# Experts of 96 slots on plain float32 weights, with the tokens in four column tiles of TensorE

## The reference, cut to what matters

```python
D_MODEL = 1024; D_FF = 2816; N_EXPERTS = 8; TOP_K = 2
def swiglu(h, wg, wu, wd):
    g = jnp.einsum('btd,df->btf', h, wg)
    u = jnp.einsum('btd,df->btf', h, wu)
    return jnp.einsum('btf,fd->btd', jax.nn.silu(g) * u, wd)
def moe(h, router, wg, wu, wd):
    logits = jnp.einsum('btd,de->bte', h, router).astype(jnp.float32)
    vals, idx = lax.top_k(logits, TOP_K)
    gates = jax.nn.softmax(vals, axis=-1)
    comb = jnp.sum(jax.nn.one_hot(idx, N_EXPERTS, dtype=jnp.float32) * gates[..., None], axis=-2)
    out = jnp.zeros_like(h)
    for e in range(N_EXPERTS):
        out = out + comb[..., e:e + 1].astype(h.dtype) * swiglu(h, wg[e], wu[e], wd[e])
    return out
```

## Time and profile before

| | us |
|---|---|
| median of 3 runs (1280.49 to 1281.12) | 1280.8 |
| the profiled execution, first to last instruction | 1280.1 |
| attention and dense layer, up to the first expert matmul | 519.2 |
| first expert | 94.4 |
| each of the experts 2 to 7 | 94.3 |
| last expert | 92.8 |
| after its last matmul | 7.9 |

### The profile page before, as it was taken

The page is one execution under the profiler, slowest core; times in us unless marked ns, Lnnn a source line. Parts: engine busy times, 40 slices in busy tenths (PEclk is TensorE's granted clock), DMA queues, the critical chain, the costliest instruction groups (busy, mean ns, idle before and its releaser), DMA issues.

```text
span 1280.1 us, 18558 instructions
## 1 busy us (share of the span) xinstructions
PE 1262.4 (99%) x6937; PEld 1026.7 (80%) x6937; DVE 934.3 (73%) x888; ACT 803.0 (63%) x813; POOL 159.1 (12%) x175
## 2 busy tenths in 40 slices
PE   7999999999999999999999999999999999999998
PEld 5476699999974656788888888888888888888886
DVE  1667544443425667888888988988988988988897
ACT  2566533333324655767867877867867867777674
POOL 4131000000001020100310300400400400300300
PEclk9999999999999999999999999999999999999999
DMA  8261375445050624999999999999999999999994
GB/s 288 42 168 34 113 250 166 164 148 181 9 186 1 133 93 160 338 359 365 376 392 356 392 386 356 394 377 374 381 382 371 385 381 357 394 374 371 387 389 170
DMA packets 124595, 350.24 MB, mean 274 GB/s; under 512 B 8401, under 2 KB 33841, under 8 KB 124545
## 3 DMA queue, kind: packets, MB, share of 16 engines
q1 hardware_dynamic: 118896, 335.55, 71.9%
q0 software_dynamic: 4096, 12.43, 3.3%
q10 hardware_dynamic: 1552, 1.56, 0.4%
HBM read 340.57 MB, written 8.95 MB: 273 GB/s over the span
## 4 chain that ended last, share of the span: by engine, by line
PE 93%; DVE 3%; DMA 2%; ACT 1%; SPq 1%; issue 0%; DVEq 0%; ACTq 0%
PE ps L2337 38%; PE ps L2357 18%; PE ps L2244 11%; PE ps L1988 8%; PE ps L2260 5%; DMA ring<-in_w_in 2%; PE ps L2345 2%; PE ps L2061 1%; PE ps L2069 1%; PE ps L2121 1%; PE ps L2136 1%; PE ps L2174 1%; PE ps L2184 1%; PE ps L2001 1%; PE ps L2416 1%; PE ps L2085 1%
## 5 line engine op out<-in xcount | busy, mean ns | idle before, releaser
L1324 DVE TENSOR_TENSOR w_lo<-ring,w_hi 128x2048 fp32r<-128x2048 f32 (+1 forms) x322 | 675.2, 2124 | 178.8 <-ACT w_hi L938 176.4
L938 ACT ACTIVATE w_hi<-ring 128x2048 fp32r<-128x2048 f32 (+1 forms) x322 | 567.3, 1781 | 212.0 <-PE ps L2357 63.3
L2337 PE MATMUL ps<-w_hi,xg_hi 128*128 128x512 f32 (+1 forms) x768 | 287.8, 375 | 0.0
L2337 PE MATMUL ps<-w_hi,xg_lo 128*128 128x512 f32 (+1 forms) x768 | 286.1, 373 | 0.0
L2337 PE MATMUL ps<-w_lo,xg_hi 128*128 128x512 f32 (+1 forms) x768 | 285.4, 372 | 0.0
L2337 PEld LDWEIGHTS ps<-w_hi,xg_hi 128*128 128x128 f32 x768 | 144.6, 188 | 25.7
L2337 PEld LDWEIGHTS ps<-w_lo,xg_hi 128*128 128x128 f32 x768 | 144.2, 188 | 25.8
L2337 PEld LDWEIGHTS ps<-w_hi,xg_lo 128*128 128x128 f32 x768 | 144.6, 188 | 24.9
L2357 PE MATMUL ps<-w_hi,am_hi 128*128 128x512 f32 x340 | 133.7, 393 | 0.0
L2357 PE MATMUL ps<-w_lo,am_hi 128*128 128x512 f32 x340 | 132.5, 390 | 0.0
L2357 PE MATMUL ps<-w_hi,am_lo 128*128 128x512 f32 x340 | 132.3, 389 | 0.0
(11 more groups left out here) (357 smaller groups left out, 1435.2 us busy)
## 6 DMA issues: line engine op xcount, KB each, us to landing
ring<-in_moe_w_down SPq DMA_DIRECT2D x80, 1024.0 KB, 8.1
ring<-in_moe_w_gate SPq DMA_DIRECT2D x64, 1024.0 KB, 9.1
ring<-in_moe_w_up SPq DMA_DIRECT2D x64, 1024.0 KB, 9.4
ring<-in_moe_w_gate SPq DMA_DIRECT2D x32, 768.0 KB, 7.5
ring<-in_moe_w_up SPq DMA_DIRECT2D x32, 768.0 KB, 5.2
ring<-in_ffn_w_gate SPq DMA_DIRECT2D x11, 1024.0 KB, 7.4
ring<-in_ffn_w_up SPq DMA_DIRECT2D x11, 1024.0 KB, 5.3
ring<-in_ffn_w_down SPq DMA_DIRECT2D x10, 1024.0 KB, 5.2
```

The costliest lines, as they stand in the source:

```text
L938: A(hi[:, 0:size], src[:, 0:size], ACT.Copy).then_inc(hi_ready, 1)
L1324: V.tensor_tensor(lo[:, 0:size], src[:, 0:size], hi[:, 0:size].bitcast(F32), ALU.subtract).then_inc(lo_ready, 1)
L2337: ins = mm_(ps[:, b + c0 // 512, 0:c1 - c0], (xg_hi, xg_lo)[xp][:, k, :], w[wp][:, k % 2, c0:c1], start=(k == 0 and n == 0), stop=(k == KD ...
```

## The change

`SLOTS` becomes 96, three groups of 32 tokens. PE no longer takes split weights: tokens (`xg`, `am`) and weights are plain float32, straight out of the ring, which has 12 slots (`MOE_RING`: the six old ones and six in the place of the split pairs) with a semaphore each (`unit_in`); `unit_used`, raised by PE, tells that a unit was read. `lanes` does one k-row: TensorE is used as four column tiles of 32. Tiles 0 to 2 hold the three token groups and run over the first three quarters of the columns (`LANE_W`: 768, 768, 640; `D_LANE`: 768); tile 3 takes the rest of the columns (`TAIL`: 256, 256, 128; `D_TAIL`: 256) for each group in turn. Results of tile 3 stand on partitions 96 to 127, one group beside the other; `turned_parts` and the copies in `output` put them where they belong. The steps `wh` and `wl` of layer 1 (the first splits of expert weights) go, and so do `moe_events`, `moe_hi_part` and `moe_lo_part`. The first expert's rows are gathered with both parts summed in one bank, and transposed once. ACT and DVE each evacuate one of the two banks of turned activations and of turned tokens. `output` and `last_output` copy the tail columns over first and then scale. The dense layer keeps its split pairs and its ring.

```diff
-SLOTS = P
+GRAN = DEC
+MAIN = P // GRAN - 1
+SLOTS = MAIN * GRAN
...
+TAIL = [w // (MAIN + 1) // P * P for w in WIDTH]
+LANE_W = [w - t for w, t in zip(WIDTH, TAIL)]
+D_TAIL = D // (MAIN + 1)
+D_LANE = D - D_TAIL
...
-DENSE_PAIRS, MOE_PAIRS = 3, 4
+DENSE_PAIRS = 3
+MOE_RING = 12
...
-            for u in range(RING):
-                slot_room(last_in_slot[(MOE_AT + u) % RING])
+            for u in range(MOE_RING):
+                if u < RING:
+                    slot_room(last_in_slot[(MOE_AT + u) % RING])
+                elif u == RING:
+                    wait_full(sp, ("o", 1, len(GROUPS) - 1))
+                    sp.wait_ge(stored, 16 * DEPTH * 10)
                 load_unit(u, 0)
...
-                    sp.wait_ge(lo_ready, j * len(EXPERT) + (ND + u - RING + 1))
+                    sp.wait_ge(unit_used, j * len(EXPERT) + (u - MOE_RING + 1))
                     load_unit(u, e)
...
                 def output():
+
                     act.wait_ge(row_moved, j + 1)
-                    act.wait_ge(y_full, j + 1)
-                    A(y_out[:, :], wide(6), ACT.Copy, scale=slot_gate[:, 0:1]).then_inc(y_taken, 1)
+                    act.wait_ge(unit_used, j * len(EXPERT) + len(EXPERT))
+                    for g in range(MAIN):
+                        ins = A(y_out[GRAN * g:GRAN * g + GRAN, D_LANE:D], wide(6)[SLOTS:P, D_TAIL * g:D_TAIL * g + D_TAIL], ACT.Copy)
+                    ins.then_inc(y_tail, 1)
+                    A(y_out[0:SLOTS, 0:D_LANE], wide(6)[0:SLOTS, 0:D_LANE], ACT.Copy, scale=slot_gate[0:SLOTS, 0:1])
+                    act.wait_ge(y_tail, j + 1)
+                    A(y_out[0:SLOTS, D_LANE:D], y_out[0:SLOTS, D_LANE:D], ACT.Copy, scale=slot_gate[0:SLOTS, 0:1]).then_inc(y_taken, 1)
...
                 def wait_unit(u):
-                    pe.wait_ge(lo_ready, j * len(EXPERT) + (ND + u + 1))
+
+                    pe.wait_ge(unit_in[u % MOE_RING], j * MOE_FILLS + 16 * (u // MOE_RING + 1))
+
+                def lanes(b, x, w, main, tail, first, last):
+
+                    for c0 in range(0, main, 512):
+                        c1 = min(c0 + 512, main)
+                        for g in range(MAIN):
+                            ins = mm_(ps[GRAN * g:GRAN * g + GRAN, b + c0 // 512, 0:c1 - c0], x[:, GRAN * g:GRAN * g + GRAN], w[:, c0:c1],
+                                      start=first, stop=last)
+                        for g in range(MAIN):
+                            at_ = tail * g
+                            if c0 <= at_ < c1:
+                                ins = mm_(ps[SLOTS:P, b + c0 // 512, at_ - c0:at_ - c0 + tail], x[:, GRAN * g:GRAN * g + GRAN],
+                                          w[:, main:main + tail], start=(first and at_ == c0),
+                                          stop=(last and (g == MAIN - 1 or at_ + tail >= c1)))
+                    return ins
...
-                    w = [x[u % MOE_PAIRS][:, 0:2 * wd].rearrange("p (k c) -> p k c", k=2) for x in (w_hi, w_lo)]
+                    w = unit_at(u)[:, 0:2 * wd].rearrange("p (k c) -> p k c", k=2)
                     for k in (2 * h, 2 * h + 1):
-                        for c0 in range(0, wd, 512):
-                            c1 = min(c0 + 512, wd)
-                            for n, (wp, xp) in enumerate(PARTS):
-                                ins = mm_(ps[:, b + c0 // 512, 0:c1 - c0], (xg_hi, xg_lo)[xp][:, k, :], w[wp][:, k % 2, c0:c1],
-                                          start=(k == 0 and n == 0), stop=(k == KD - 1 and n == 2))
-                    in_use(ins, u)
+                        ins = lanes(0 if kind == "gate" else 2, xg[:, k, :], w[:, k % 2, :], LANE_W[c], TAIL[c], k == 0, k == KD - 1)
+                    ins.then_inc(unit_used, 1)
```

More of the change, by code:

```diff
@@ L200, in expert_plan @@
     return order + [("down", c, h) for c in (1, 2) for h in range(4)]
[L203 to L225, removed]
 def ffn_jobs():
@@ L442, in build @@
         w_ready = [sem(f"w_ready{i}") for i in range(RING)]
+        unit_in = [sem(f"unit_in{i}") for i in range(MOE_RING)]
+        unit_used = sem("unit_used")
         small_full = [sem(f"small_full{i}") for i in range(3)]
@@ L634, in build @@
         SPLIT_AT = (2, 3, 5)
-        DOWN_USED = 10
         def wait_pair(eng, n):
@@ L647, in dense_size, with unit_at @@
             return SLOT_W if key[0] != "down" or key[2] < 5 else SLOT_W // 2
[L649 to L667, removed]
+        def unit_at(u):
+            i = u % MOE_RING
+            return ring[:, (MOE_AT + i) % RING, :] if i < RING else ring_more[i - RING][:, :]
         GAINS_IN = 16 * len(GAIN)
@@ L944, in dense_hi_part @@
                 split_hi(ring[:, slot_of[key], :], n, w_hi[n % DENSE_PAIRS], dense_size(key))
[L946 to L954, removed]
-                split_hi(ring[:, s, :], u, w_hi[u % MOE_PAIRS], moe_size(u))
             def squares(l, t, where):
@@ L1278, in last_output @@
+                    act.wait_ge(y_tail, j + 1)
+                    A(y_out[0:SLOTS, D_LANE:D], y_out[0:SLOTS, D_LANE:D], ACT.Copy, scale=slot_gate[0:SLOTS, 0:1]).then_inc(y_taken, 1)
                 def last_output():
                     act.wait_ge(row_moved, j + 1)
-                    for half in range(2):
-                        act.wait_ge(y_half, half + 1)
-                        A(y_hi[:, 512 * half:512 * half + 512], ps[:, 6 + half, :], ACT.Copy, scale=slot_gate[:, 0:1]).then_inc(y_high, 1)
@@ L1284, in expert @@
-                for u in range(MOE_PAIRS, len(EXPERT) + MOE_PAIRS):
-                    for what, c in MOE_EVENTS.get(u, ()):
-                        if what == "silu":
-                            silu(c)
-                        elif what == "turned":
-                            chunk_high(c)
-                        elif what == "tokens" and not final:
-                            tokens_high(j + 2)
-                        elif what == "output":
-                            if final:
-                                last_output()
-                            else:
-                                output()
-                    if u < len(EXPERT) or not final:
-                        moe_hi_part(j, u)
+                    act.wait_ge(y_half, 1)
@@ new lines, in last_output @@
+                    act.wait_ge(y_tail, j + 1)
+                    A(y_hi[0:SLOTS, D_LANE:D], y_out[0:SLOTS, D_LANE:D], ACT.Copy, scale=slot_gate[0:SLOTS, 0:1]).then_inc(y_high, 1)
+                silu(0)
+                turned(0)
+                silu(1)
+                turned(1)
+                silu(2)
+                if not final:
+                    act.wait_ge(xgT_full, j + 2)
+                    tokens_first_half(j + 2, 4)
+                turned(2)
+                if final:
+                    last_output()
+                else:
+                    output()
@@ L1656, in _ @@
                     elif kind == "wl":
-                        if l == 0:
-                            dense_lo_part(which[0])
-                        else:
-                            moe_lo_part(0, which[0], first=True)
+                        dense_lo_part(which[0])
                     elif kind == "nb":
@@ new lines, in activations, with turned @@
+                    V.tensor_tensor(act_m[:, 0:LANE_W[c]], sgm[:, 0:LANE_W[c]], wide(2)[:, 0:LANE_W[c]], ALU.mult).then_inc(act_done, 1)
+                def turned(c):
+                    dve.wait_ge(aT_full, j * CHUNKS + (c + 1))
+                    for dst, src in turned_parts(c, 1):
+                        ins = V.tensor_copy(dst, src)
+                    ins.then_inc(aT_second, 1)
+                if not final:
+                    picks(bass.ds(j + 1, 1))
+                activations(0)
@@ L1811, in _ @@
+                if not final:
+                    dve.wait_ge(row_moved, j + 1)
+                    table(j + 2)
+                turned(0)
+                activations(1)
+                turned(1)
+                activations(2)
+                if not final:
+                    dve.wait_ge(xgT_full, j + 2)
+                    tokens_second_half(5)
+                turned(2)
             last = dve.snap(more * NE + (NE - 1))
```

252 lines of the change are left out of this document (115 added, 137 removed), and 8 rows, old and new, of tables (ACT_ORDER, DVE_ORDER).

## The result

The changed kernel takes **1301.7 us** (median of 4 runs, 1301.1 to 1303.3) against 1280.6 for the kernel before on the same chip: 1.0168 times as long, 95% interval 1.0153 to 1.0182. It is 1.7% slower, where 1271.6 was forecast. Its profiled execution spans 1299.6 us.

The account below looks back on a forecast made before the run. PE was taken to bound the experts, in its own matmuls. 1280.1 - 25.2 - 0.5 + 0.3 + 16.2 = 1270.9, and 0.7 for the median of runs gave 1271.6 us, range 1252 to 1294.

Parts of the forecast that it names:

- the turn of the loop: PE's return to the head of its longer expert loop: 2.7 us for each of six, +16.2 us, at most 3.9 each.
- seven passes without the turn, each: PE's matmuls, transposes and table for one expert: 91.2 us, 3.1 less than before.
- the experts without turns: Seven passes and the last: 727.8 us against 753.0, so -25.2 us.
- start of the experts: Eight transposes go, but the second half waits for ACT's copy: -0.5 us, between -0.9 and 0.
- end: After the last matmul, a tail copy and another ACT and DVE step: +0.3 us, between 0 and 1.5.
- Four column tiles: In PE's expert matmuls, four tiles run 3.8 times at once, as equal tiles in the earlier trace did.
- rival 4: Expert matmuls: tiles of unequal length overlap less, 4.3 us a pass per 5% lost, 1306 us at 5%; chance 0.07.
- Rival 2: At loop turns PE stands idle and its clock falls: 5.5 us a turn, 1288.4 us, slower than before; chance 0.19.
- Rival 1: PE's loop turn costs nothing, store large enough or head fetched ahead: 1255.4 us; chance 0.17.
- Transfers: Expert weight stream needs 86 to 91 us a pass: cost 0, up to +2 us a pass.
- rival 3: Weight stream becomes the bound at 378 GB/s, no pass shorter than 93.7 us: 1277 us; chance 0.11.
- Splits: ACT's and DVE's split copies go: nothing gained in steady passes, 0 in the attention layer's tail.

Follow-up runs that it names:

- experiment 4: Changed kernel with column-tile matmuls left out, PE loop bodies of 1,196, 1,484, 1,772 and 1,932 instructions: 1254.8, 1256.2, 1300.4 and 1300.2 us.
- Experiments 1: Changed kernel with PE's seven turns of the expert loop written out one after the other instead of a hardware loop: 1256.4 us.
- experiment 6: Kernel before with two experts in PE's loop body (1,920 instructions), first and last expert outside the loop, two returns: 1288.0 us.
- experiment 7: Changed kernel with PE's expert loop written out and a ring of 6 weight chunks instead of 12: 1259.7 us.
- experiment 3: Changed kernel with two experts in PE's loop body, first and last expert outside the loop, two returns instead of six: 1274.5 us.
- experiments 2: Changed kernel with the loop kept and a hint for its closing branch (hint_back_edge=True): 1269.5 us.
- experiment 9: Changed kernel for any number of rounds, seven experts written out, then two endings, the usual one reached without a taken branch: 1258.6 us.

## Why the prediction was wrong

**The step that failed is the turn of the loop**, and within it the price. Measured against its own sum:

| term | forecast, us | measured, us |
|---|---|---|
| seven passes without the turn, each | 91.2 | 91.40 |
| the experts without turns | -25.2 | -23.3 |
| the turn, six times | 16.2 (2.7 each, bound 3.9) | 44.8 (7.5 each) |
| start of the experts | -0.5 | -0.6 |
| end | +0.3 | +0.3 |
| attention layers | 0 | -1.7 |
| sum | 1270.9 | 1299.6 |

- **That PE bounds the experts**, and the working of the pass, held: k-rows of 1,024 columns start 1.295 us apart (1.29 forecast), those of 768 1.077 (1.075). The chain of the changed kernel in rows of 768:

```profile
681.00 0.50 PE ps L2297 x6
682.08 0.50 PE ps L2297 x6
683.16 0.50 PE ps L2297 x6
```

- **Four column tiles.** The 3.8 times of the earlier trace rows carried over, and rival 4 is dead: more than half of the products cost 0.26 us (experiment 4).
- **The turn, that it costs.** The chain of reasoning was right up to here: the growth of the body, the packets of 16 KB, the missing queue in the steady passes all said that this body might not be held. Experiments 1 and 4 show it.
- **The turn, what it costs.** I priced it as a small transfer's 2.7 us, 16.2 in all, and it cost 44.8. From the packet's start to the next matmul it is 2.6 to 2.8, 16.1 in all. That this piece agrees is luck: the row was of a transfer of 128 KB, the piece is a packet of 1.0 to 1.1 us and 1.6 to 1.7 us behind it. Missing from the price are the 1.9 to 2.9 us that PE stands before the packet starts, 13.9 in all; why they grow from pass to pass stays open. And 3.9 was no upper bound, since it was built from transfers alone, with nothing for the branch itself.
- **The clock** is the second missed piece, some 13.4 us. Rival 2 had the mechanism, PE idle and then at half clock as at the end of the trace before (PE through at 1274.9, clock 0.50 in 1277 to 1280), and gave it 0.19. It priced a turn at 5.5 us and the kernel at 1288; it is 7.5 and 1301.7. The reason against it, that short gaps in the attention layers left the clock whole (1.4 us ahead of 25.8 and of 29.2, clock 1.00), held for the gaps of 2.3 us in experiment 6 and not for those of 4.6.
- **Rival 1**, 1255.4 with no cost of the turn, is what experiment 1 measured: 1256.4.
- **Transfers**, 0 to +2 us a pass, were 0 (experiments 1 and 7); rival 3 didn't come up.
- **Splits, start, end** were right to within 0.1 us where they can be told apart. The 1.7 us that the attention layers were shorter is no effect of the splits: experiment 3, with the same code up to the experts, had only 0.3 of it. The starts of all these kernels scatter by 2 us from layer 0 on.

The weak place was not the missing row but the width left around it. A cost that is paid six times and appears nowhere in the trace had bounds of 0 and 3.9 us, while 4.2 us already turned the sign. The 26% for slower rested on two rivals instead of on this term.

## What to carry to other kernels

Count the instructions of each engine's loop body before and after a change: up to 1,484 PE returned free of charge here, from 1,772 on a return of the changed kernel cost some 7 us, of which about a third was the half clock behind the gap, and with 1,920 a return of the kernel before cost 2.6 us. If the body must be longer, write the turns out and let the usual case fall through every branch (1256.4 and 1258.6 us against 1301.7); a hint on the closing branch keeps most of the gain (1269.5) where code can't be written out. A gap called "issue" at the head of a loop, 4.6 to 5.6 us in the changed kernel, with one packet of the instruction queue in it, is the sign.

## What the runs showed of the hardware

- A return that misses takes 2.6 to 2.9 us from the packet's start to the next matmul in both kernels with one packet in the gap (3.4 us from the second of two packets in experiment 3). PE stands idle 4.6 to 5.6 us in the changed one and 2.3 to 2.4 us in the kernel before, where the packet starts while PE is still multiplying.
- In the experts, with PE idle for 4.5 us or more, the granted clock read 0.50 for 3.4 or 6.8 us from within the gap or just behind it; with PE idle for 2.3 to 2.5 us it didn't. At the start of the kernel idle time alone doesn't tell: PE stands for 2.4 to 3.4 us from 4.2 us on in all 14 profiled executions, and in six of them the clock read 0.50 from some 8 us on, the longest gap, 3.4 us in experiment 7, not being among these. In experiments 2 and 4 the clock also read 0.50 for 3.4 us where the experts begin, without such a gap; why there and not in the others stays open.
- The miss is all or nothing in the changed kernel: none with 1,484 instructions, the whole cost with 1,772. Written out in a straight line, 2,604 instructions a pass were fetched at no cost that shows (passes of 91.40 us, 91.14 to 91.17 with bodies that stayed).
- A jump forward over 2,604 instructions, right behind the reading of the number that decided it, cost 6.7 us of idle and a shorter gap behind it, some 10 us in all where a return cost 7.5; a branch not taken cost nothing that shows (passes of 91.39 to 91.40 us in experiment 9).
